# A transformer block's start and its MLP's side work: loads, group sums, scales and one turn are put in another order

## The reference

```python
for i in range(DEPTH):                       # 2 layers
    ml = split((silu(c) @ w_mod[i] + b_mod[i]), 6)      # shift, scale, gate, twice; latent
    mc = split((silu(c_ctx) @ w_mod[i] + b_mod[i]), 6)  # the same for the context
    hl = rms_norm(xl, g) * (1 + ml[1]) + ml[0]
    hc = rms_norm(xc, g) * (1 + mc[1]) + mc[0]
    # even layer: Fourier mixing + neighbourhood attention; odd layer: differential attention,
    # with lam = exp(sum(lq1*lk1)) - exp(sum(lq2*lk2)) + lam_init
    yl, yc = mixer(hl, hc)
    xl = xl + ml[2] * yl
    xl = xl + ml[5] * squared_relu_mlp(modulate(xl, g2, ml[3], ml[4]), w_mlp_in, w_mlp_out)
    ...                                      # the context likewise, except in the last layer
return rms_norm(xl, final_norm_g)
```

## Time and profile before

| | |
|---|---|
| median of 3 runs | 1687.19 us (1685.81 to 1687.30) |
| the profiled execution's own time | 1685.71 us |
| its span | 1683.9 us |
| TensorE busy in the span | 1627.0 us, 97% |
| VectorE, ScalarE, GpSimd busy | 887.0, 520.6, 613.9 us |
| mean granted TensorE clock | 0.987 of full speed |

### The profile page before, as it was taken

One profiled execution on the slowest core, in us unless ns is written; L12 is line 12 of the kernel. 1 busy time (PEld: TensorE's weight loads), 2 busy tenths in 40 slices (PEclk: granted clock), 3 DMA queues, 4 the chain that ended last, 5 costly groups with the idle time before them and its releaser, 6 DMA issues.

```text
span 1683.9 us, 23840 instructions
## 1 busy us (share of the span) xinstructions
PE 1627.0 (97%) x9350; PEld 1365.0 (81%) x9350; DVE 887.0 (53%) x1176; ACT 520.6 (31%) x924; POOL 613.9 (36%) x392
## 2 busy tenths in 40 slices
PE   5899989999899999999999999999999999999997
PEld 2777878888788888888888888877857988888886
DVE  2400207627963872783585668319964744435264
ACT  3422337524211211121121422138852522222221
POOL 1422256324432332332322433345502644444441
PEclk9999999999999999999999999999999999999998
DMA  9373121312342242324232122200001232222221
GB/s 366 141 255 146 64 70 50 126 51 69 103 167 70 93 166 85 100 100 137 82 132 100 52 87 88 76 14 1 24 16 63 90 101 98 100 88 99 100 76 50
DMA packets 49484, 163.97 MB, mean 97 GB/s; under 512 B 6376, under 2 KB 6632, under 8 KB 45808
## 3 DMA queue, kind: packets, MB, share of 16 engines
q1 hardware_dynamic: 49392, 162.68, 27.9%
HBM read 159.77 MB, written 2.10 MB: 96 GB/s over the span
## 4 chain that ended last, share of the span: by engine, by line
PE 92%; DVE 4%; ACT 1%; issue 1%; DMA 1%; POOL 1%; SPq 0%; DVEq 0%; ACTq 0%
PE ps L1485 26%; PE ps L1486 26%; PE ps L1487 26%; PE ps L1936 2%; PE ps L1898 2%; PE ps L1925 1%; PE ps L1806 1%; PE ps L1796 1%; PE ps L1680 1%; PE ps L1834 1%; DMA xc<-ctx_dram 1%; DVE h L1150 1%; PE ps L1829 1%; PE ps L1692 0%; DVE tmp_a L1143 0%
## 5 line engine op out<-in xcount | busy, mean ns | idle before, releaser
L540 POOL TENSOR_TENSOR w_lo<-raw,w_hi 128x1024 fp32r<-128x1024 f32 (+1 forms) x228 | 482.2, 2125 | 916.4 <-ACT w_hi L689 916.4
L1485 PE MATMUL ps<-h,w_hi 128*128 128x512 f32 (+1 forms) x1176 | 413.8, 352 | 6.0 <-DVE h L1150 5.0
L1486 PE MATMUL ps<-h,w_lo 128*128 128x512 f32 (+1 forms) x1176 | 412.0, 350 | 0.0
L1487 PE MATMUL ps<-h,w_hi 128*128 128x512 f32 (+1 forms) x1176 | 409.6, 348 | 0.0
L689 ACT ACTIVATE w_hi<-raw 128x1024 fp32r<-128x1024 f32 x189 | 200.0, 1058 | 401.7 <-PE ps L1487 395.7
L1485 PE MATMUL ps<-hid_lo,w_hi 128*128 128x512 f32 (+1 forms) x800 | 279.3, 349 | 0.0
L1486 PE MATMUL ps<-hid_hi,w_lo 128*128 128x512 f32 (+1 forms) x800 | 278.9, 349 | 0.0
L1487 PE MATMUL ps<-hid_hi,w_hi 128*128 128x512 f32 (+1 forms) x800 | 277.2, 346 | 0.0
L1485 PEld LDWEIGHTS ps<-h,w_hi 128*128 128x128 f32 x1176 | 223.2, 190 | 45.2 <-issue 11.7
L1487 PEld LDWEIGHTS ps<-h,w_hi 128*128 128x128 f32 x1176 | 222.3, 189 | 30.3
L1486 PEld LDWEIGHTS ps<-h,w_lo 128*128 128x128 f32 x1176 | 223.1, 190 | 28.4
(11 more groups left out here) (203 smaller groups left out, 2183.9 us busy)
## 6 DMA issues: line engine op xcount, KB each, us to landing
raw<-units_dram SPq DMA_DIRECT2D x189, 512.0 KB, 3.3
mod_ring<-w_mod_dram SPq DMA_DIRECT2D x96, 256.0 KB, 3.3
mod_big<-w_mod_dram SPq DMA_DIRECT2D x16, 1024.0 KB, 8.7
mod_late<-w_mod_dram SPq DMA_DIRECT2D x8, 1024.0 KB, 6.1
xl<-x_dram SPq DMA_DIRECT2D x2, 2048.0 KB, 11.5
bias<-bias_dram SPq DMA_DIRECT2D x8, 384.0 KB, 3.6
xc<-ctx_dram SPq DMA_DIRECT2D x2, 1024.0 KB, 13.4
out_dram<-out_t SPq DMA_DIRECT2D x8, 256.0 KB, 2.9
```

The costliest lines, as they stand in the source:

```text
L540: ins = nc.gpsimd.tensor_tensor(w_lo[:, s, sl], raw[:, s, sl], w_hi[:, s, sl].bitcast(F32), op=ALU.subtract)
L1485: mm(out, a[0], b[1], start=start, stop=False)
L1486: mm(out, a[1], b[0], start=False, stop=False)
L1487: return mm(out, a[0], b[0], start=False, stop=stop)
```

## The change

In the head: SP issues `cond` and chunks 0 and 1 first, then three constants, x and ctx, the other three constants, chunk 2, and, after its wait, chunk 3. The Exp of c waits for `cond` alone. The lambda product, its sum and its Exp come after chunks 0 and 1, and wait for six constants. ScalarE takes a Sqrt of one element per partition before the squares. TensorE does `half_turn(2)` before `half_mm(3)` and `half_turn(3)` before the spreads. ScalarE does `half_rows(3)` before it rounds units 0 to 2. `scales(0)` is done in two halves, for chunks 2 and 3, each in one instruction. GpSimd's first three `low` are done in four pieces.

In the MLP: chunk 0's turn stands after unit 5 (was 4), chunk 1's steps stand at units 5 and 6 (were 4 and 5). Chunk 0's steps (0, 1), chunk 1's turn (8) and chunk 2 (8, 9, turn 12) stay. TensorE's extra wait ahead of the turn in the first block is dropped.

```diff
-MOD_AT = {4 * j: (j, range(0, 4)) for j in range(3)}
-MOD_AT |= {4 * j + 1: (j, range(4, 8)) for j in range(3)}
-MOD_TURN = {4: 0, 8: 1, 12: 2}
+MOD_AT = {i: (j, range(0, 4)) for j, i in enumerate((0, 5, 8))}
+MOD_AT |= {i: (j, range(4, 8)) for j, i in enumerate((1, 6, 9))}
+MOD_TURN = {5: 0, 8: 1, 12: 2}
...
         def _(sp):
-            for dst, name in ((cond, "cond"), (ident, "ident"), (b_mod, "b_mod"), (gains, "gains"),
-                              (mask, "mask"), (lam_in, "lam"), (subg, "subln")):
-                sp.dma_start(dst[:], t[name]).then_inc(consts_in, 16)
...
-            for m in range(4):
-                if m == 3:
-                    sp.wait_ge(half_summed, 1)
-                load_half_mod(m)
-                if m == 1:
-                    sp.dma_start(xl[:], t["x"]).then_inc(x_in, 16)
-                    sp.dma_start(xc[:], t["ctx"]).then_inc(x_in, 16)
+            sp.dma_start(cond[:], t["cond"]).then_inc(cond_in, 16)
+            load_half_mod(0)
+            load_half_mod(1)
+            for dst, name in ((ident, "ident"), (lam_in, "lam"), (b_mod, "b_mod")):
+                sp.dma_start(dst[:], t[name]).then_inc(consts_in, 16)
+            sp.dma_start(xl[:], t["x"]).then_inc(x_in, 16)
+            sp.dma_start(xc[:], t["ctx"]).then_inc(x_in, 16)
+            for dst, name in ((gains, "gains"), (mask, "mask"), (subg, "subln")):
+                sp.dma_start(dst[:], t[name]).then_inc(consts_in, 16)
+            load_half_mod(2)
+            sp.wait_ge(half_summed, 1)
+            load_half_mod(3)
...
             for u in range(AHEAD):
-                low(u, u)
+                low(u, u, 4)
...
-            act.wait_ge(consts_in, 16 * 7)
+            act.wait_ge(cond_in, 16)
             nc.scalar.activation(ctmp[:], cond[:], ACT.Exp, scale=-1.0).then_inc(exp_c, 1)
-
-            act.wait_ge(lam_mm, 1)
-            nc.scalar.activation(lam_t[:, 2:4], ps[:, 6, 0:2], ACT.Exp).then_inc(lam_exp, 1)
...
             half_rows(0)
             half_rows(1)
+            act.wait_ge(lam_mm, 1)
+            nc.scalar.activation(lam_t[:, 2:4], ps[:, 6, 0:2], ACT.Exp).then_inc(lam_exp, 1)
+            act.wait_ge(ones_ok, 1)
+            nc.scalar.activation(stat[:, 63:64], eps_c[:, 0:1], ACT.Sqrt)
             act.wait_ge(x_in, 32)
...
             norm_root(0, 1)
+            half_rows(3)
             high_u(0)
             high_u(1)
-            half_rows(3)
             high_u(2)
...
-            def scales(i):
+            def scales(i, halves=(0, 1)):
                 m = 12 * (i // 2) + 2 * (1 + 3 * (i % 2))
-                dve.wait_ge(mod_done, m + 2 if i < 2 else 24)
-                for v in range(2 if i < 3 else 1):
-                    ins = V.scalar_tensor_tensor(out=gs[:, i, v].rearrange("p (a b) -> p a b", a=2),
-                                                 in0=mods[:, m:m + 2, v, :], scalar=1.0,
-                                                 in1=gains[:, i].rearrange("p (a b) -> p a b", a=2),
-                                                 op0=ALU.add, op1=ALU.mult)
-                st.wait(ins)
+                vs = 2 if i < 3 else 1
+                for a in halves:
+                    dve.wait_ge(mod_done, m + a + 1 if i < 2 else 24)
+                    st.wait(V.scalar_tensor_tensor(out=gs[:, i, 0:vs, 4 * a:4 * a + 4], in0=mods[:, m + a, 0:vs, :], scalar=1.0,
+                                                   in1=gains[:, i, 4 * a:4 * a + 4].unsqueeze(1).broadcast_to([P, vs, 4]),
+                                                   op0=ALU.add, op1=ALU.mult))
...
             dve.sem_inc(ones_ok, 1)
-            dve.wait_ge(consts_in, 16 * 7)
-            lam = lam_in[:].rearrange("p (a b) -> p a b", b=2)
-            tt(lam_t[0:HD, 0:2], lam[:, :, 0], lam[:, :, 1], op=ALU.mult).then_inc(lam_ok, 1)
...
             V.tensor_copy(cact_wide[:, :, 0:2], cact[:]).then_inc(cact_ok, 1)
+            dve.wait_ge(consts_in, 16 * 6)
+            lam = lam_in[:].rearrange("p (a b) -> p a b", b=2)
+            tt(lam_t[0:HD, 0:2], lam[:, :, 0], lam[:, :, 1], op=ALU.mult).then_inc(lam_ok, 1)
...
             half_add(0)
+            dve.wait_ge(lam_exp, 1)
+
+            st.wait(V.scalar_tensor_tensor(out=lam_t[:, 4:5], in0=lam_t[:, 3:4], scalar=LAM_INIT,
+                                           in1=lam_t[:, 2:3], op0=ALU.subtract, op1=ALU.subtract))
...
             half_add(2)
+            scales(0, (0,))
             half_add(3)
-            scales(0)
+            scales(0, (1,))
...
                         if layer == 0 and i in MOD_TURN:
-                            if first and i == 4:
-                                pe.wait_ge(relu_made, ha(0, 0, 3))
                             mod_mm(b, MOD_TURN[i])
...
             half_mm(0)
             half_mm(1)
+            pe.wait_ge(ones_ok, 1)
+            pe.wait_ge(lam_ok, 1)
+            mm(ps[:, 6, 0:2], ones[0:HD, :], lam_t[0:HD, 0:2], start=True, stop=True).then_inc(lam_mm, 1)
             half_turn(0)
             half_mm(2)
             half_turn(1)
+            pe.wait_ge(lam_exp, 1)
             norm_sums(0, 0)
             norm_sums(0, 1)
+            half_turn(2)
             half_mm(3)
+            half_turn(3)
             norm_spread(0, 0)
             norm_spread(0, 1)
-            half_turn(2)
-            half_turn(3)
             pe.wait_ge(mod_done, 4)
```

More of the change, by code:

```diff
@@ L243, in sem @@
             return ctx.enter_context(nc.semaphore(name))
+        cond_in = sem("cond_in")
         consts_in = sem("consts_in")
@@ L1285, in _ @@
             V.tensor_copy(cact_wide[:, :, 0:2], cact[:]).then_inc(cact_ok, 1)
+            dve.wait_ge(consts_in, 16 * 6)
+            lam = lam_in[:].rearrange("p (a b) -> p a b", b=2)
+            tt(lam_t[0:HD, 0:2], lam[:, :, 0], lam[:, :, 1], op=ALU.mult).then_inc(lam_ok, 1)
             V.tensor_reduce(group_sum[:], ident[:].rearrange("p (g v) -> p v g", g=4)[:, 0:2], AX.X, ALU.add).then_inc(group_ok, 1)
             V.tensor_scalar(subg[:, 1:2], subg[:, 0:1], 1.0 - LAM_INIT, None, ALU.mult)
-            dve.wait_ge(lam_exp, 1)
-            st.wait(V.scalar_tensor_tensor(out=lam_t[:, 4:5], in0=lam_t[:, 3:4], scalar=LAM_INIT,
-                                           in1=lam_t[:, 2:3], op0=ALU.subtract, op1=ALU.subtract))
             def half_add(m):
@@ L1662, in mlp @@
                     norm_spread(4, 1)
-            pe.wait_ge(ones_ok, 1)
-            pe.wait_ge(lam_ok, 1)
-            mm(ps[:, 6, 0:2], ones[0:HD, :], lam_t[0:HD, 0:2], start=True, stop=True).then_inc(lam_mm, 1)
             def half_mm(m):
```

## The result

The changed kernel takes 1691.87 us (median of 8 runs, 1690.48 to 1693.67), the kernel before 1686.61 (8 runs, 1684.58 to 1687.59): ratio 1.0039, 95% interval [1.003, 1.0048], slower (the quotient of these two medians is 1.0031). I had forecast 1688.7 and no change. The profiled execution of after took 1690.48 us, its span 1688.7, 4.8 more than before, where I had +1.5. Ratios come from repeated runs; the time of a single step comes from one profiled execution.

What follows compares the result with a forecast made beforehand. TensorE's matmul work was taken as the bound (busy 1627.0 of 1683.9 us), so only its waits counted. Head -1.8, first MLP block -0.2, later blocks +3.5 made +1.5: 1687.2 profiled, 1688.7 median, range 1683.0 to 1693.0.

Steps and rivals of the forecast that it cites:

- (a): Head, loads: the first modulation chunk is issued 3.1 us earlier; ctx lands at 21.4 (bounds 21.0 and 21.9).
- (b): Head: the lambda product waits for constants behind x and ctx, landing about 21.75; squares start at 24.35, 0.2 us later.
- (c): Head, after the norm sums: the new TensorE order gives 41.8 for the first spread, against 41.14 for the last group sum before.
- (d): Head: the scales' 2.24 us stall goes, t_part starts at 41.85, not 43.65; first h matmul 44.8 against 46.08, -1.3.
- (e): Head, after the first h matmul: unit 1's low part and the clock decide; the head gains 1.0 or 2.4, taken as -1.8.
- The MLP: MLP: the first block's wait of 4.76 becomes 4.5 (-0.2 us); blocks 1 to 3 newly wait on hidden 7, together +3.5.
- Rival 1: MLP: the late wait is simply gone, hidden 7 in time in every block; 1678.5, or to 1683 with a remainder; chance 0.14.
- Rival 2: MLP: later blocks' stalls are a GpSimd hold longer, +2.1 in each of three blocks; 1695, or 1691 with one; chance 0.18.
- The sum: Whole kernel: head, first MLP block and later blocks add to +1.5 us on the profiled execution; median 1688.7.
- the head's -1.8: Whole head: a gain of 1.8 us, with bounds +0.4 and -4.5.
- Rival 3: Head loses: squares at 24.8 or later, h_low held by several pieces, clock down; +0.4 in the head, 1690.9; chance 0.06.

Runs made afterwards that it cites:

- early lambda wait: Changed kernel, but the lambda product waits only for the three constants ahead of x; the late three have their own semaphore: 1688.04 us, ratio 1.0017.
- spread tables: Kernel before, chunk 1's second four steps moved behind hidden(7): with chunk 0's turn after unit 5, 1678.31 us; with it kept after unit 4, 1686.0 us.

## Why the prediction was wrong

**(a) Issue and landing: right in kind, 0.6 us off.** ctx lands at about 22.0 (the squares start at 21.87 to 22.05 in the four kernels with the early lambda wait), where I had 21.4 and a bound of 21.9.

**(b) The new wait: right in mechanism, too small in size.** I had the last constants 0.35 us behind ctx, at 21.75, and the product there; it ran at 22.67, some 0.65 behind ctx. From there to the squares I had 2.6 us and the trace has 2.5 (22.67 to 25.15). The squares came at 25.15, outside my bound of 24.8. By the 2.66 us of the Trainium skill (ScalarE: Activation LUTs, What ACT_TABLE_LOAD costs) they would have come later still; the trace has the load at 23.75 for 1.28 us and the Sqrt at 25.04, so the row was the right figure. The run with the wait taken away gave 3.1 us, so (b)'s reading, that it eats the earlier issue and that the squares could have followed ctx, holds.

**(c) The step that failed: the durations after the sums.** I took a gain of 2.0 us between the squares and t_part (0.2 later, then 1.8 earlier; my terms add to 41.66 and not 41.8 for the first spread, which changes little). For it I let the sums end as long after the squares as before (they took 1.50 there) and took one group sum at half of the two in the earlier trace rows, 0.9. At the clock granted there the sums took 2.69 and group sum 2 cost 1.78 (36.57 to 38.35). That makes them 1.2 and 0.9 longer; with 0.8 from (a) and (b) and 0.1 from `half_mm(3)` it is the 3.0 us by which t_part missed (44.85, not 41.85). I wrote of the clock only for the time after the first h matmul and took over durations from stretches granted 0.76 to 1.00, without a bound for them. It also hid an argument against the order: a group sum ahead of `half_mm(3)` adds to the path in front of the last piece of work, where two behind it cost 1.84 together. The old order and place gave 0.2% back in runs.

A part of these 3.0 us belongs to the one execution that the earlier trace rows show, and not to the change. The other three profiles with the head of before (MLP alone, and both spread tables in it) have the first h matmul at 46.88, 46.78 and 46.69, not 46.08, and a granted clock of 0.50 from 24 to 36, where before's profile had 1.00, 1.00 and 0.82. The kernel with the MLP's edits alone:
```profile
24.51 0.63 ACT L707 ACTIVATE tmp_b<-xl 128x512 f32<-128x512 f32 x1 [4.87 <-DMA xc<-ctx_dram]
...
33.30 2.72 PE L1536 MATMUL ps<-ones,ssum 128*128 128x1 f32 x12
...
42.86 1.55 DVE L1090 SCALAR_TENSOR_TENSOR gs<-mods,gains 128x8 f32<-128x8 f32 x2
44.45 1.41 DVE L1143 SCALAR_TENSOR_TENSOR tmp_a<-xl,gs,ps 128x512 f32<-128x512 f32 x2
...
46.88 0.76 PE L1485 MATMUL ps<-h,w_hi 128*128 128x512 f32 x1 [4.26 <-DVE h L1150]
```
Against it the squares of the changed kernel are 0.6 later, squares to t_part take 0.2 less (19.70, 19.94), and t_part to the first h matmul 0.6 more (2.99, 2.43): 1.0 later in all, where I had 1.3 earlier. The slow sums stand in both and drop out. Of the 2.0 that I had between squares and t_part, 0.9 went to group sum 2, 0.2 to `half_mm(3)` (3.7 from its start to ScalarE's copy, where I had 3.5), and 0.7 were never there: the scales' stall is 1.55 here, 1.43 and 1.81 in the other two profiles, and I took the 2.24 of one.

**(d) Scales, `half_rows(3)`, low parts: right, but for the size of the stall.** No stall of 2 us; t_part to the first h matmul took 2.99 us, forecast 2.95. GpSimd's start at 43.68 against a forecast of 40.9 is the 3.0 us shift of all of it, and as priced it costs `h_low` 0.4 to 0.6 us each.

**(e) After the first h matmul: not decided.** To the first Relu after it was 0.3 us shorter than before (374.20, 374.50), forecast 0.5; but the three other profiles with the head of before have 374.75, 373.38 and 374.41, so 0.3 says nothing.

**The MLP: right in mechanism, and in size in this profile.** The late wait took the early one's place: 4.27 us where I had 4.5, then 1.04, 0.99 and 0.75 where I had 1.25, 1.25 and 1.0. `hidden(7)` of block 1 ended at 617.69 (616.73 + 0.96), forecast 616.3, and 1.36 of the difference was there when the block began. Rival 1 was wrong by VectorE's order, and the spread tables show the condition that I had given it, VectorE at `hidden(7)` before 472.3: there it ends at 471.34 and the wait is gone. Rival 2's extra hold of GpSimd came in no block.

**The sum.** In the pair of profiles the MLP's +3.3 was met (-0.10 + 1.31 + 1.24 + 0.9); the head's -1.8 was +1.46. Repeated runs are less clear. The MLP alone costs 0.31 to 0.58% there, 5.2 to 9.8 us, and the changed kernel is 0.25%, 4.2 us, above the head alone; the first is clear of 3.3 (its own profile shows 3.9 behind the first Relu), and what the rest is wasn't found. The head costs 0.8 to 4 us beside the MLP of before and nothing that can be seen beside the changed one. So the total is sure, and its division is not. Rival 3, the head loses, is what the profiles show (squares at 25.15, `h_low` beside several pieces, the low clock), at a price above the +0.4 that I gave it, because the durations above weren't in it. The time, 1691.87, lies in the range; the "no change" doesn't hold, since the MLP's cost alone is near the 0.2% bound and I counted on the head to offset part of it. That the time is only 3.2 us above the forecast is no merit of the head's sum, which had the wrong sign.

## What to carry to other kernels

The lambda product needed one small transfer and waited for six, the last of them behind 3 MB: it ran at 22.67, and at 14.71 once the late three had a semaphore of their own. If a consumer needs only some transfers of a group, split the group before moving the rest behind megabytes. Moving work off the point where an engine waits pays only if the engine that makes the operand has slack at the next point too; here the turn and the steps behind it one unit later are worth 0.4% with four steps moved past `hidden(7)` and cost 0.25% (in the changed kernel) to 0.44% (on the head of before) without. Before a small matmul is moved, read the granted clock of its new place, and look at more than one execution of it, of the kernel before too: the row that a forecast rests on may be the odd one.

## What the runs showed of the hardware

The granted clock in the head differs between executions of the same instructions, as above, and twelve matmuls of one column take 2.69 to 2.72 us at 0.50 to 0.54, 1.50 in before's profile (0.82). With filler matmuls it was 1.00 in 20 to 24 and 0.50 in 28 to 32, as shown above. Such a difference is seen far from the edit too, from 1260 to 1280 us: before, and the kernel with the early lambda wait, whose work there is the same but runs 1.4 us later:
```profile
1260.00:1280.00 20.00, 20.00 (x56) 10.85 (x55) 12.28 (x15) 5.30 (x7) 1.44 (x1) 0.83 0.00 1
```
```profile
1260.00:1280.00 20.00, 19.83 (x42) 9.61 (x40) 10.73 (x13) 4.44 (x7) 0.00 (x0) 0.66 0.00 0
```
From the first Relu of block 3 to the end that profile is 3.4 us longer than before's (860.2 against 856.8). By the starts of ScalarE's instructions 0.85 of it is there when the MLP ends, and the other 2.7 come between 1265 and 1272 us (of before's time). The profile of the kernel with the old order loses 2.8 there too, the changed kernel's nothing. One profiled execution thus can't settle a difference of 2 us over the whole span; the steps inside it, and the repeated runs, can.
